# Moving the sums of weight quarters forward in the DMA slots of a hybrid encoder layer, and two small steps on VectorE with them

## The chip, the core and the metric

The kernel runs on one core of a Trainium2 chip. The core has TensorE (matrix products, results in PSUM), VectorE, ScalarE and GpSimd (elementwise work; GpSimd can't read PSUM), and SyncE, whose queue here issues nearly all loads. Each engine works off its own queue strictly in order and waits on semaphores. Transfers that SyncE, ScalarE and GpSimd issue run on the same 16 DMA engines. The metric is the time of one execution on the device, in microseconds.

## What is computed

One step of a hybrid encoder layer for 512 prompt frames and 32 frames of a running stream (544 tokens), width 1024, all in float32, followed by a final norm:

```python
xn = rms_norm(x, g_mix)
u, q, k, v, gates = split(xn @ w_in)
gate_a, gate_b = split(sigmoid(gates + b_gate))
y_pool = (causal_mean_2_4_8_16(u) - u) @ w_pool_grp * pool_scale     # 4 groups of 128 channels
y_sb   = stick_breaking_attention(q, k, v)                            # 8 heads x 64, strictly causal
x = x + (gate_a * (y_pool @ w_pool_up) + gate_b * (y_sb @ w_sb_up)) @ w_out
x = x + square(relu(rms_norm(x, g_mlp) @ w_up)) @ w_down              # hidden width 4096
x = x + sigmoid(rms_norm(x, g_ple) @ w_ple_gate) * (p @ w_ple_proj)
y = rms_norm(x, g_final)
```

## The kernel before

Activations lie with features on partitions and the 544 tokens as columns, in two halves of 272. Every float32 product is made of three products of rounded parts: high x high, low x high and high x low. ScalarE rounds a weight tile (128 x 1024) into `w_hi` (`split`, `hi`, lines 845 and 853), VectorE makes `w_lo` as the difference (1812, 1820). Three tiles are prepared ahead of TensorE, in a ring of four; the raw tiles come through a ring of two buffers in the attention stage and of six later, loaded by SyncE as soon as VectorE has made the low part of the buffer's last tile.

The attention stage is four pairs of heads (`pair`), so eight heads, each over one psum area of scores. For head g, VectorE adds the positive part of the scores to a logarithm ("stick", line 1898), GpSimd masks the four diagonal blocks (`mask_diagonals`, 767), ScalarE rounds, VectorE makes the low part, TensorE forms the sums along keys, ScalarE takes the exponential, GpSimd masks again, the two parts are made again (943, 1919) and TensorE forms the outputs (1420). In the last pair ScalarE has in addition the eight sigmoids of `gate_a` between two changes of its function table, and the rounding of the pooling means. The four pooling groups run through VectorE and ScalarE too: `group_hi` (957) and `group_lo` (1985) empty a result slot in PSUM, and the first pooling product, `pool_part(0)`, uses the slot that group 2 had.

The MLP and the gate after it use Strassen-Winograd products: for each group of weight columns seven products instead of eight. Four of the seven weight tiles are sums of quarters, S1 to S4, which the DMA engines make in device memory: `SUM_STEPS` has four copies in step 0, then two, one and one accumulating transfers in steps 1 to 3, eight transfers for each of 16 groups. `sum_slot(k)` says which groups are at which step in slot k: group i begins in slot i. GpSimd issues slot k's transfers (`sum_copies`, `sum_additions`, lines 782 and 789), for k up to 7 behind the second mask of head k, later when TensorE reaches certain products (`paces`). Before slot k's first transfer it waits until all transfers of the slots before have landed (`sums_made(k - 1)`). SyncE waits, before it loads a sum, until the group's four slots are through.

In the MLP's first group TensorE makes product s = 0 to 6 (A11, S1, S2, S4, S3, A12, A22). ScalarE copies the results of s = 0, 1, 2 out of PSUM (`copy_quarter`, 1097), VectorE adds those of s = 3, 4, 5 (`add_quarter`, 2190) and scales the quarters by the norm's reciprocal root (2214, 2200, 2219). The mean square for that norm is a product with ones (`statistics`, 1657), made behind s = 2; VectorE turns it into a variance (1840), ScalarE takes logarithm and exponential (874, 876, `root`), and VectorE adds a step of Newton (1846 to 1848, `root_step`). Results go through four PSUM slots; product s = 5 writes into the slot of s = 3, once VectorE has added that.

Of the kernel before, what the change touches and what calls it, by code (L numbers as in the profile page):

```python
# [19 lines left out]
HEADS = 8  # L20
# [69 lines left out]
SUM_GROUPS = tuple((what, 2 * c + e) for c in range(CHUNKS) for what in ("up", "dn") if what == "up" or c < SEVENS  # L90
                   for e in range(2)) + (("ple", 0), ("ple", 1))

SUM_PAD = 16

X_QUARTER = {"A11": (0, 0), "S1": (1, 1), "S2": (0, 1), "S4": (0, 1), "S3": (1, 1), "A12": (0, 0), "A22": (1, 0)}
# [17 lines left out]

def stage_results():

    seq = [(("out", q), result_slot(N_OUT + q), False) for q in range(KT)]

    def group(stage, g, pair, stat=None):  # L120
        for s in range(T_UP):
            seq.append(((stage, g, s), 2 * pair + (not IN_X[s]), BY_ACT[s]))
            if s == 2 and stat:
                seq.append(((stat,), 2 * (1 - pair), False))

    for c in range(CHUNKS):
        group("up", 2 * c, 0, "stat1" if c == 0 else None)
        group("up", 2 * c + 1, 1)
        if c < SEVENS:
            seq.extend((("dn", c, s, e), 2 * e + (not IN_X[s]), False) for s in range(T_UP) for e in range(2))  # L130
        else:
            seq.extend((("down", c, q), q % 4, False) for q in range(KT))
    group("ple", 0, 0, "stat2")
    seq.extend((("proj", q), (2 + q) % 4, False) for q in range(KT // 2))

    for what in LAST_ORDER:
        if what[0] == "ple":
            seq.append((what, 2 + (not IN_X[what[2]]), BY_ACT[what[2]]))
        else:
            seq.append((what, {"pj": what[-1], "stat3": 3 * what[-1]}[what[0]], False))  # L140
    return seq
# [156 lines left out]
def hybrid_step_kernel(nc, w_tiles, x_t, p_t, ck_t, cv, state_t, w_grp, vecs,  # L298
# [5 lines left out]
    with ctx:  # L304
# [316 lines left out]

        def sum_slot(k):

            return [(i, k - i) for i in range(max(0, k - len(SUM_STEPS) + 1), min(k + 1, len(SUM_GROUPS)))]

        def sums_made(k):

            return 16 * sum(len(SUM_STEPS[step]) for j in range(k + 1) for _, step in sum_slot(j))
# [8 lines left out]
        def _(sp):  # L637
# [35 lines left out]
            def staged(n):  # L673
                name = STAGED_LOADS[n]
                wait_free(n)
                group, what = group_side(name) or (None, None)
                if what in SUMS:
                    nth = SUM_GROUPS.index(group)
                    sp.wait_ge(sums_in, sums_made(nth + len(SUM_STEPS) - 1))
                    sp.dma_start(raw_buf(n), sums_t[len(SUMS) * nth + SUMS.index(what), :, :])\  # L680
                        .then_inc(raw_in[raw_at(n)], 16)
                elif name[0] == "p":
                    sp.dma_start(raw_buf(n)[:, 0:TOK], p_t[:, name[1], :]).then_inc(raw_in[raw_at(n)], 16)
                else:
                    sp.dma_start(raw_buf(n), w_tiles[stored_tile(name), :, :]).then_inc(raw_in[raw_at(n)], 16)
# [21 lines left out]
        def _(pool):  # L707
# [104 lines left out]
            for c in range(CHUNKS):  # L812
                second = [NTH[("dn", c, s, 0)] for s in (0, 4)] if c < SEVENS else [NTH[("down", c, q)] for q in (0, 4)]
                paces += [(NTH[("up", 2 * c, 0)], NTH[("up", 2 * c + 1, 0)]), tuple(second)]
            for k, (copies, additions) in enumerate(paces, HEADS):
                if copies:
                    pool.wait_ge(full, copies)
                sum_copies(k)
                if copies:
                    pool.wait_ge(full, additions)  # L820
                sum_additions(k)
# [11 lines left out]
        def _(act):  # L833
# [306 lines left out]
            def up_seven(g):  # L1140

                for s in range(T_UP):
# [17 lines left out]
                        act.wait_ge(sum_done, nth_t(g - 1, "T4"))  # L1160
                    if g and s == 2:
                        act.wait_ge(olo_done, nth_lo(g - 1, "T3"))
                    if BY_ACT[s]:
                        copy_quarter(g, n, s)
                    if s == 0 and g % 2 == 1:
# [4 lines left out]
                    if s == 6:  # L1170
                        act.wait_ge(rel_done, 2 * g + 2)
                        square_hi(g, "B11")
                    if g == 0 and s == 3:
                        act.wait_ge(taken, taken_count(NTH[("stat1",)]))
                        root(2)

            def up_group(g):
                for s in range(T_UP):
# [144 lines left out]
        def _(pe):  # L1323
# [337 lines left out]
            def group_of(stage, g, tiles, made_by=None, stat=None, n_squares=0):  # L1661
                for s in range(T_UP):
                    product_of(tiles + s, NTH[(stage, g, s)], s, made_by).then_inc(full, 1)
                    if s == 2 and stat:
                        statistics(stat, n_squares)

            def down(c):
# [131 lines left out]
        def _(dve):  # L1799
# [189 lines left out]
            def pair(i):  # L1989
# [69 lines left out]
                if last:  # L2059
                    group_lo(1)  # L2060
                    mean_lo(2)
                    mean_lo(3)
                    gate(3, i)
                else:
                    split(AHEAD + 7, i, S1_PER)
                stick(1, i)
                if last:
                    group_lo(2)
                    group_lo(3)
                    stick_later(1, i)  # L2070
                    split(AHEAD + 7, i, S1_PER)
# [195 lines left out]

            def group_step(g, s):

                if s == 3 and g == 0:  # L2270
                    statistics("stat1")
                if SIDES[s] in ("S4", "S3", "A12"):
                    add_quarter(g, NTH[("up", g, s)], s)
                if s == 3 and g == 0:
                    root_step(2)
                if SIDES[s] == "S3":
                    scaled_second(g, "S3")
                if SIDES[s] == "A12":
                    scaled_first(g)
# [274 lines left out]
```

## Time and profile before

| | us |
|---|---|
| median of 3 runs | 772.89 |
| lowest, highest | 772.16, 772.94 |
| the profiled execution | 772.34 |
| its span, first to last instruction | 770.6 |

The granted TensorE clock is 0.996 of full speed over the span. The span is what the profile shows; the device time contains 1.7 us more around it. In the rows below an instruction's start is given in us from the start of the span, its length in us, the engine, the line of the kernel, and at the end in brackets how long the engine had been idle and what released it. Consecutive instructions of one kind are one row. DMA shares say how much of the time of all 16 engines the packets of a queue took; overlapping packets can bring a short stretch above 100%.

### The profile page before, as it was taken

The numbers are of one execution on the slowest core, as the hardware profiler recorded it, in microseconds if no ns is written. First come the engines' busy times: TensorE is split into PE (matmuls) and PEld (weight loads), VectorE is DVE, ScalarE is ACT, GpSimd is POOL, SyncE is SP. The second block draws the span as 40 slices with busy tenths as digits, with TensorE's granted clock in tenths as the row PEclk, the third lists the DMA queues.
The fourth block names the chain that finished last, engine by engine and source line by source line (L and its number), as shares of the span: only waits on it lengthen the run. The fifth ranks groups of instructions, "written<-read, shape, count | busy, mean of one in ns | idle before, by whom it ended". The sixth has DMA issues, their size and how long they took to land.

```text
span 770.6 us, 14459 instructions
## 1 busy us (share of the span) xinstructions
PE 754.8 (98%) x5902; PEld 746.2 (97%) x5902; DVE 556.9 (72%) x705; ACT 422.0 (55%) x524; POOL 147.2 (19%) x259
## 2 busy tenths in 40 slices
PE   9999999999999999999999999999999999999994
PEld 9999999999999999999999999999999999999993
DVE  6776556566567527588998669965998667677986
ACT  7545535435485442477674347634763356556575
POOL 1051342453471332021110111111101000000001
PEclk9999999999999999999999999999999999999998
DMA  7254848769779899988797989789776957342503
GB/s 242 93 181 140 233 147 224 225 193 262 218 179 265 259 242 275 292 267 262 213 299 270 236 329 251 282 232 354 207 243 201 278 185 217 105 117 66 204 1 116
DMA packets 49516, 165.78 MB, mean 215 GB/s; under 512 B 6320, under 2 KB 8368, under 8 KB 49456
## 3 DMA queue, kind: packets, MB, share of 16 engines
q1 hardware_dynamic: 28512, 94.16, 35.6%
q0 software_dynamic: 18688, 67.18, 35.5%
q10 hardware_dynamic: 2256, 3.60, 1.4%
q8 instruction: 43, 0.70, 0.4%
q14 instruction: 17, 0.14, 0.1%
HBM read 160.39 MB, written 71.63 MB: 301 GB/s over the span
## 4 chain that ended last, share of the span: by engine, by line
PE 90%; DVE 5%; ACT 3%; issue 1%; DMA 1%; SPq 0%; POOL 0%; POOLq 0%; DVEq 0%
PE psum L1646 23%; PE psum L1697 16%; PE psum L1345 14%; PE psum L1351 14%; PE psum L1348 14%; PE psum L1394 1%; PE psum L1422 1%; DMA xt<-x_t 1%; PE psum L1420 1%; PE psum L1382 1%; PE psum L1381 1%; ACT xt L1265 1%; PE psum L1401 1%; PE psum L1406 1%; ACT L879 0%
## 5 line engine op out<-in xcount | busy, mean ns | idle before, releaser
L853 ACT ACTIVATE w_hi<-raw_more 128x1024 fp32r<-128x1024 f32 x83 | 87.7, 1056 | 72.3 <-PE psum L1697 43.3
L1345 PE MATMUL psum<-a_hi,w_hi 128*128 128x272 f32 x576 | 120.6, 291 | 0.6 <-DVE w_lo L1812 0.5
L1820 DVE TENSOR_TENSOR w_lo<-raw_more,w_hi 128x1024 fp32r<-128x1024 f32 x83 | 101.1, 1222 | 26.1 <-ACT w_hi L853 25.7
L1351 PE MATMUL psum<-a_hi,w_lo 128*128 128x272 f32 x576 | 119.3, 289 | 0.0
L1348 PE MATMUL psum<-a_lo,w_hi 128*128 128x272 f32 x576 | 118.9, 288 | 0.0
L1646 PE MATMUL psum<-u_hi,w_hi 128*128 128x272 f32 x560 | 116.4, 289 | 1.0 <-ACT h_of L1097 1.0
L1646 PE MATMUL psum<-u_hi,w_lo 128*128 128x272 f32 x560 | 115.8, 289 | 0.0
L1646 PE MATMUL psum<-u_lo,w_hi 128*128 128x272 f32 x560 | 115.7, 288 | 0.0
L1345 PEld LDWEIGHTS psum<-a_hi,w_hi 128*128 128x128 f32 x576 | 90.3, 189 | 1.1 <-DVE w_lo L1812 0.7
L1348 PEld LDWEIGHTS psum<-a_lo,w_hi 128*128 128x128 f32 x576 | 90.5, 189 | 0.0
L1351 PEld LDWEIGHTS psum<-a_hi,w_lo 128*128 128x128 f32 x576 | 90.0, 189 | 0.0
L1646 PEld LDWEIGHTS psum<-u_hi,w_hi 128*128 128x128 f32 x560 | 87.9, 188 | 1.7 <-issue 1.2
L1646 PEld LDWEIGHTS psum<-u_lo,w_hi 128*128 128x128 f32 x560 | 88.3, 189 | 0.0
L1646 PEld LDWEIGHTS psum<-u_hi,w_lo 128*128 128x128 f32 x560 | 87.4, 188 | 0.0
L1812 DVE TENSOR_TENSOR w_lo<-raw,w_hi 128x1024 fp32r<-128x1024 f32 x41 | 51.2, 1250 | 43.3 <-ACT w_hi L845 43.1
L1820 DVE TENSOR_TENSOR w_lo<-raw,w_hi 128x1024 fp32r<-128x1024 f32 x44 | 53.6, 1222 | 19.2 <-ACT w_hi L853 12.3
L789 POOL DMA_DIRECT2D sums_t<-sums_t x32 | 27.5, 1013 | 207.1 <-PE psum L1646 87.9
L1348 PE MATMUL psum<-b_lo,w_hi 128*128 128x272 f32 x304 | 62.9, 288 | 0.0
L853 ACT ACTIVATE w_hi<-raw 128x1024 fp32r<-128x1024 f32 x39 | 41.2, 1056 | 36.0 <-PE psum L1697 21.6
L1345 PE MATMUL psum<-b_hi,w_hi 128*128 128x272 f32 x288 | 60.0, 290 | 0.0
L782 POOL DMA_DIRECT2D sums_t<-w_tiles x64 | 33.6, 535 | 135.5 <-DMA sums_t<-w_tiles 97.7
L1351 PE MATMUL psum<-b_hi,w_lo 128*128 128x272 f32 x288 | 59.4, 287 | 0.0
(287 smaller groups left out, 1553.0 us busy)
## 6 DMA issues: line engine op xcount, KB each, us to landing
sums_t<-w_tiles POOLq DMA_DIRECT2D x96, 512.0 KB, 8.2
raw<-w_tiles SPq DMA_DIRECT2D x63, 512.0 KB, 4.4
raw_more<-sums_t SPq DMA_DIRECT2D x42, 512.0 KB, 5.8
raw_more<-w_tiles SPq DMA_DIRECT2D x41, 512.0 KB, 4.5
sums_t<-sums_t POOLq DMA_DIRECT2D x32, 512.0 KB, 11.1
raw<-sums_t SPq DMA_DIRECT2D x22, 512.0 KB, 6.0
xt<-x_t SPq DMA_DIRECT2D x8, 272.0 KB, 5.7
y_t<-xt SPq DMA_DIRECT2D x16, 136.0 KB, 1.9
```

The costliest lines, as they stand in the source:

```text
L782: pool.dma_start(sum_tile(i, what), sum_tile(i, of)).then_inc(sums_in, 16)
L789: pool.dma_start(sum_tile(i, what), sum_tile(i, of), accum_op=ALU.add).then_inc(sums_in, 16)
L853: act.activation(w_hi[:, t % W_RING, :, :].rearrange("p k c -> p (k c)"), src, ACT.Copy)\
L1265: act.activation(x, x, ACT.Copy, scale=g_fin[:, m:m + 1]).then_inc(xg_last, 1)
L1345: pe.matmul(base[:, h, :], w_hi[:, s, wk, :], at(hi, k, h * HALF, (h + 1) * HALF), start=(opens and q == 0), stop=False, skip_group_check= ...
L1348: pe.matmul(base[:, h, :], w_hi[:, s, wk, :], at(lo, k, h * HALF, (h + 1) * HALF), start=False, stop=False, skip_group_check=True)
L1351: mm = pe.matmul(base[:, h, :], w_lo[:, s, wk, :], at(hi, k, h * HALF, (h + 1) * HALF), start=False, stop=(closes and q == len(ks) - 1), s ...
L1381: pe.matmul(z, b_lo[:, keys], b_hi[:, both], start=(b != 3), stop=False, skip_group_check=True)
L1646: mm = pe.matmul(out[:, two, :], w_part[:, t % W_RING, 2 * k + two, :], u_part[:, op, k, :], start=(OPENS[s] and k == 0 and w_part is w_hi ...
L1697: mm = pe.matmul(out[:, two, :], w_part[:, t % W_RING, 2 * k + two, :], h_part[:, i * HALF:(i + 1) * HALF], start=(OPENS[s] and k == 0 and ...
L1812: dve.tensor_tensor(w_lo[:, s, :, :].rearrange("p k c -> p (k c)"), raw[:, t % RAW_RING, :], w_hi[:, s, :, :].rearrange("p k c -> p (k c)" ...
L1820: dve.tensor_tensor(w_lo[:, t % W_RING, :, :].rearrange("p k c -> p (k c)"), src, w_hi[:, t % W_RING, :, :].rearrange("p k c -> p (k c)"), ...
```

## The change

There are three parts.

1. `BEGINS` says in which slot each group of sums begins: 0, 1, 2, 2, 3, 3, 4, 5, 5, 7, 9, 11, 12, 13, 14, 15. Nine groups instead of six begin in slots 0 to 5. SyncE's wait for a group follows it.
2. In the last pair, `group_lo(2)` stands ahead of the last stick instead of behind it.
3. The mean square of the MLP's norm is made behind s = 1. ScalarE's root stands ahead of its copy of S2's result, VectorE's variance at the end of s = 2, and `root_step(2)` ahead of the addition of S4's result.

```diff
+BEGINS = (0, 1, 2, 2, 3, 3, 4, 5, 5, 7, 9, 11, 12, 13, 14, 15)
+SLOTS = BEGINS[-1] + len(SUM_STEPS)
...
+STAT_BEHIND = {"stat1": 1, "stat2": 2}
...
-            if s == 2 and stat:
+            if s == STAT_BEHIND.get(stat):
...
-            return [(i, k - i) for i in range(max(0, k - len(SUM_STEPS) + 1), min(k + 1, len(SUM_GROUPS)))]
+            return [(i, k - at) for i, at in enumerate(BEGINS) if 0 <= k - at < len(SUM_STEPS)]
...
-                    sp.wait_ge(sums_in, sums_made(nth + len(SUM_STEPS) - 1))
+                    sp.wait_ge(sums_in, sums_made(BEGINS[nth] + len(SUM_STEPS) - 1))
...
-            for k, (copies, additions) in enumerate(paces, HEADS):
+            for k, (copies, additions) in zip(range(HEADS, SLOTS), paces):
...
+                    if g == 0 and s == 2:
+                        act.wait_ge(taken, taken_count(NTH[("stat1",)]))
+                        root(2)
                     if BY_ACT[s]:
                         copy_quarter(g, n, s)
...
-                    if g == 0 and s == 3:
-                        act.wait_ge(taken, taken_count(NTH[("stat1",)]))
-                        root(2)
...
+                if last:
+
+                    group_lo(2)
                 stick(1, i)
                 if last:
-                    group_lo(2)
                     group_lo(3)
...
+                if s == 2 and g == 0:
+                    statistics("stat1")
                 if s == 3 and g == 0:
-                    statistics("stat1")
+                    root_step(2)
                 if SIDES[s] in ("S4", "S3", "A12"):
                     add_quarter(g, NTH[("up", g, s)], s)
-                if s == 3 and g == 0:
-                    root_step(2)
```

GpSimd from the second mask of head 4 to the issue of slot 5, in the kernel before. `sums_t` holds the sums; a transfer from `w_tiles` on the first DMA line is a copy, those on the second are additions; `gates` and `upad` are the window mean:

```order
L767 AFFINE_SELECT work<-work 128x128 x4
L782 DMA sums_t<-w_tiles 128x1024 x4
L789 DMA sums_t<-sums_t 128x1024 x2
L789 DMA sums_t<-w_tiles 128x1024 x2
L757 TENSOR_SCALAR gates<-gates 128x551
L758 TENSOR_TENSOR gates<-gates,invc 128x8
L760 TENSOR_TENSOR upad<-gates,upad 128x559
L767 AFFINE_SELECT work<-work 128x128 x8
L782 DMA sums_t<-w_tiles 128x1024 x4
L789 DMA sums_t<-sums_t 128x1024 x2
L789 DMA sums_t<-w_tiles 128x1024 x2
```

and in the changed one, with the line numbers moved by 8:

```order
L775 AFFINE_SELECT work<-work 128x128 x4
L790 DMA sums_t<-w_tiles 128x1024 x4
L797 DMA sums_t<-sums_t 128x1024 x3
L797 DMA sums_t<-w_tiles 128x1024 x4
L765 TENSOR_SCALAR gates<-gates 128x551
L766 TENSOR_TENSOR gates<-gates,invc 128x8
L768 TENSOR_TENSOR upad<-gates,upad 128x559
L775 AFFINE_SELECT work<-work 128x128 x8
L790 DMA sums_t<-w_tiles 128x1024 x8
L797 DMA sums_t<-sums_t 128x1024 x4
L797 DMA sums_t<-w_tiles 128x1024 x2
```

Slot 4 grows from 4 copies and 4 additions to 4 and 7, slot 5 to 8 and 6 (the other slots of the first eight follow from `BEGINS`).

ScalarE at the MLP's first group. `w_hi` is a weight rounding, `h_of` the copy of a result, `ev` logarithm and exponential. Before:

```order
L853 ACTIVATE w_hi<-raw 128x1024
L1097 ACTIVATE h_of<-psum 128x2x272
L853 ACTIVATE w_hi<-raw 128x1024
L1097 ACTIVATE h_of<-psum 128x2x272
L853 ACTIVATE w_hi<-raw_more 128x1024
L874 ACTIVATE ev<-work 128x544
L876 ACTIVATE ev<-ev 128x544
L853 ACTIVATE w_hi<-raw_more 128x1024 x2
```

and now:

```order
L861 ACTIVATE w_hi<-raw 128x1024
L1105 ACTIVATE h_of<-psum 128x2x272
L861 ACTIVATE w_hi<-raw 128x1024
L882 ACTIVATE ev<-work 128x544
L884 ACTIVATE ev<-ev 128x544
L1105 ACTIVATE h_of<-psum 128x2x272
L861 ACTIVATE w_hi<-raw_more 128x1024 x3
```

The two functions moved ahead of the copy and of the rounding of the tile for s = 6.

VectorE at the same place, before (`w_lo` a weight's low part, `work<-psum` the variance, `ev` and `rn` the step of Newton, `h_of` with `psum` an addition of a result):

```order
L1820 TENSOR_TENSOR w_lo<-raw,w_hi 128x1024 x2
L1820 TENSOR_TENSOR w_lo<-raw_more,w_hi 128x1024
L1840 TENSOR_SCALAR work<-psum 128x544
L2190 TENSOR_TENSOR h_of<-h_of,psum 128x2x272
L1846 SCALAR_TENSOR_TENSOR ev<-ev 128x544
L1847 TENSOR_TENSOR ev<-ev,work 128x544
L1848 SCALAR_TENSOR_TENSOR rn<-ev 128x544
L1820 TENSOR_TENSOR w_lo<-raw_more,w_hi 128x1024
L2190 TENSOR_TENSOR h_of<-h_of,psum 128x2x272
L2214 SCALAR_TENSOR_TENSOR h_of<-h_of,rn 128x2x272
```

and now:

```order
L1828 TENSOR_TENSOR w_lo<-raw,w_hi 128x1024 x2
L1848 TENSOR_SCALAR work<-psum 128x544
L1828 TENSOR_TENSOR w_lo<-raw_more,w_hi 128x1024
L1854 SCALAR_TENSOR_TENSOR ev<-ev 128x544
L1855 TENSOR_TENSOR ev<-ev,work 128x544
L1856 SCALAR_TENSOR_TENSOR rn<-ev 128x544
L2200 TENSOR_TENSOR h_of<-h_of,psum 128x2x272
L1828 TENSOR_TENSOR w_lo<-raw_more,w_hi 128x1024
L2200 TENSOR_TENSOR h_of<-h_of,psum 128x2x272
L2224 SCALAR_TENSOR_TENSOR h_of<-h_of,rn 128x2x272
```

The variance moved ahead of one low part, and the three steps of the root ahead of the first addition.

## Rows read from the trace of the kernel before

**Rows 1.** the page's part 1: busy us, share of the span, instructions
```profile
PE 754.8 (98%) x5902; PEld 746.2 (97%) x5902; DVE 556.9 (72%) x705; ACT 422.0 (55%) x524; POOL 147.2 (19%) x259
```

**Rows 2.** instructions in order of time, TensorE; [idle before <-releaser] at the end
```profile
245.09 0.49 PE L1345 MATMUL psum<-mean_hi,w_hi 128*128 128x272 f32 x2 [1.11 <-issue]
...
384.42 0.49 PE L1646 MATMUL psum<-u_hi,w_hi 128*128 128x272 f32 x2 [1.02 <-ACT h_of L1097]
```

**Rows 3.** in order of time, GpSimd, 139 to 229 us (L767: masks)
```profile
140.45 2.15 POOL L782 DMA_DIRECT2D sums_t<-w_tiles  x4
...
169.95 2.09 POOL L782 DMA_DIRECT2D sums_t<-w_tiles  x4
...
174.18 2.92 POOL L757 TENSOR_SCALAR gates<-gates 128x551 f32<-128x551 f32 x1
...
183.69 1.03 POOL L767 TENSOR_SCALAR_AFFINE_SELECT work<-work 128x128 f32<-128x128 f32 x4 [5.16 <-DVE work L1898]
...
210.60 1.95 POOL L767 TENSOR_SCALAR_AFFINE_SELECT work<-work 128x128 f32<-128x128 f32 x4 [6.14 <-DVE work L1898]
```

**Rows 4.** DMA queues (q0 GpSimd's, q1 SyncE's): 260:262, 152:156, 162:170, 140:170 us
```profile
q0 software_dynamic: 206, 0.76, 101.1%
...
q0 software_dynamic: 237, 0.84, 107.5%
...
q0 software_dynamic: 40, 0.01, 0.8%
...
q0 software_dynamic: 1216, 4.21, 57.0%
q1 hardware_dynamic: 576, 2.10, 20.2%
```

**Rows 5.** in order of time, ScalarE, 212 to 229 us
```profile
212.58 1.27 ACT L930 ACTIVATE b_hi<-work 128x1280 fp32r<-128x1280 f32 x1 [2.62 <-POOL work L767]
...
228.41 1.27 ACT L943 ACTIVATE b_hi<-work 128x1280 fp32r<-128x1280 f32 x1 [0.19 <-POOL work L767]
```

**Rows 6.** stretch: us, ScalarE busy (x instructions), clock, DMA share, GB/s
```profile
214.10:228.20 14.10, 13.91 (x20) 1.00 0.62 166
```

**Rows 7.** in order of time, VectorE, then TensorE, 230 to 233 us
```profile
230.81 1.48 DVE L1919 TENSOR_TENSOR b_lo<-work,b_hi 128x1280 fp32r<-128x1280 f32 x1
...
232.67 0.39 PE L1420 MATMUL psum<-b_hi 128*128 128x512 f32 x1
```

**Rows 8.** in order of time, GpSimd, then TensorE, 267 to 269 us
```profile
267.74 0.44 POOL L807 TENSOR_SCALAR_AFFINE_SELECT work<-work 32x256 f32<-32x256 f32 x1 [6.18 <-DVE work L2111]
...
268.34 0.59 PE L1559 MATMUL psum<-work,negtri 128*128 128x256 f32 x2
```

**Rows 9.** in order of time, VectorE, then ScalarE, 242 to 246 us
```profile
242.82 1.48 DVE L1898 SCALAR_TENSOR_TENSOR work<-psum,work 128x1280 f32<-128x1280 f32 x1
244.21 1.47 DVE L1985 SCALAR_TENSOR_TENSOR b_lo<-psum,vec,b_hi 128x544 fp32r<-128x544 f32 x2
...
242.93 0.72 ACT L957 ACTIVATE b_hi<-psum,vec 128x544 fp32r<-128x544 f32 x1 [0.74 <-PE psum L1328]
```

**Rows 10.** in order of time, VectorE, then ScalarE, 361 to 376 us
```profile
362.56 2.36 DVE L1820 TENSOR_TENSOR w_lo<-raw,w_hi 128x1024 fp32r<-128x1024 f32 x2
366.10 1.23 DVE L1820 TENSOR_TENSOR w_lo<-raw_more,w_hi 128x1024 fp32r<-128x1024 f32 x1 [1.19 <-ACT w_hi L853]
367.24 0.72 DVE L1840 TENSOR_SCALAR work<-psum 128x544 f32<-128x544 f32 x1
...
369.38 0.73 DVE L1846 SCALAR_TENSOR_TENSOR ev<-ev 128x544 f32<-128x544 f32 x1 [0.16 <-ACT ev L876]
...
373.55 0.72 DVE L2214 SCALAR_TENSOR_TENSOR h_of<-h_of,rn 128x544 f32<-128x544 f32 x1
...
365.02 1.05 ACT L853 ACTIVATE w_hi<-raw_more 128x1024 fp32r<-128x1024 f32 x1
368.00 0.66 ACT L874 ACTIVATE ev<-work 128x544 f32<-128x544 f32 x1 [1.93 <-DVE work L1840]
```

More of the change, by code:

```diff
@@ L1663, in group_of @@
                     product_of(tiles + s, NTH[(stage, g, s)], s, made_by).then_inc(full, 1)
-                    if s == 2 and stat:
+                    if s == STAT_BEHIND.get(stat):
                         statistics(stat, n_squares)
```

## The prediction, made before the changed kernel ran

> **What bounds the kernel now.** Read the busy shares first: TensorE is busy 98% of the span, VectorE 72%, ScalarE 55%, GpSimd 19% [rows 1]. So a change can only give back one of TensorE's few gaps, or open new ones. Then TensorE's waits, and for the two of about 1 us that aren't at the start or the end its rows in order of time [rows 2]: 1.11 us in front of the first product after the last attention pair (start 245.09), 1.02 us in front of a product of the second MLP group (start 384.42). The second and third part of the change can be worth these two gaps, 2.1 us or 0.27%, and no more. The first part, the sums of weight quarters begun earlier, frees no engine that TensorE waits for; its gain can only be zero, and what it can cost has to be looked for on GpSimd's queue, since the copies and additions are issued there, between the masks that attention needs.
>
> **First part: sums begun earlier.** The 128 transfers stay the same; they move between slots. By the start numbers the slots 0 to 7 hold 4, 6, 11, 14, 11, 14, 7 and 7 transfers, where they held 4, 6, 7, 8, 8, 8, 8 and 8. GpSimd begins slot k behind the second mask of head k, and first waits until every transfer of slots before k has landed. A slot is one head long: slot 3 is begun at 140.45, slot 4 at 169.95, 29.5 us later [rows 3].
> What a transfer takes: when only copies are in the queue, 0.76 MB move in 2 us at a 101% share of the 16 DMA engines [rows 4], so the 0.524 MB of one take 1.38 us. When only additions are in it, 0.84 MB move in 4 us at a share over 100%, so one takes 2.5 us, 2.6 with the ragged ends. The engines are full in both cases, so more transfers in the queue don't make them faster. Over the 30 us of slot 3 GpSimd's queue took 57% and the weight loads 20% of the engines, and it was empty from 162.3 on (0.01 MB after 162) [rows 4]. That is 21.85 us from 140.45, which leaves 7.6 us to spare.
> Slot 3 in the new order has 4 copies and 2 additions more: 4 x 1.38 + 2 x 2.6 = 10.7 us of engine time; with the loads taking a fifth of the engines (0.21) that is 10.7 / 0.79 = 13.5 us. It ends at 162.3 + 13.5 = 175.8 where GpSimd asks at 169.95. GpSimd is held for 5.85 us. Slot 4 has 3 additions more, 7.8 / 0.79 = 9.9: it ends at 175.8 + 21.85 + 9.9 = 207.55. Slot 5 then issues 14 transfers; eight took 4.23 us (169.95 to 174.18 [rows 3]), 0.53 each, so 7.4 us: GpSimd is free for the next mask at 214.95.
> Behind the waiting instruction stand the masks. At head 5 the mask is due at 183.69 [rows 3]; GpSimd would come to it at 175.8 + 11 x 0.53 = 181.6, and a window mean of some 4 us stands in between (it begins behind the last issue, at 174.18 before): about 2 us late. Some of it reaches TensorE, an estimated 0.8 us, since the outputs of head 5 use the masked values one head later with less than that to spare. At head 6 it is due at 210.60 [rows 3] and comes at 214.95. The mask ended at 212.55 and ScalarE took it up at 212.58 after 2.62 us of waiting; alone on the SBUF it takes about 1.0 us (four selects) and ends at 215.95, 3.4 us late. From there ScalarE has no air: of the 14.1 us up to 228.2 it is busy 13.91 [rows 6], with eight sigmoids and two table loads, and what follows, the rounding of the probabilities at 228.41, waited for nothing but 0.19 us of mask [rows 5]. VectorE's low part of them starts at 230.81, takes 1.49, and TensorE reads it at 232.67 [rows 7]: 0.4 us to spare. So 3.0 us of the 3.4 arrive at TensorE; the 0.8 of head 5 is contained in them, since this chain hangs on GpSimd's time and not on TensorE's.
> Slot 5 (14 transfers again) ends at 207.55 + 21.85 + 13.5 = 242.9. Slot 6 is 7 additions: 18.2, and 6 for start and loads (21.85 less 4 x 1.38 + 4 x 2.6), and about 2.2 for the 1 MB of cached keys and values loaded in it, so it ends near 269.3. Slot 7's issue takes 7 x 0.53 = 3.7 more: 273.0. The mask of the running stream's scores, due at 267.74, is read by TensorE at 268.34 [rows 8]. It will be due at 267.74 + 3.0 - 0.5 = 270.25 and comes 2.75 later; 0.15 is slack: 2.6 us. After that no work of GpSimd's is awaited until the end, and the fuller slots are over. Together 5.6 us. Bounds: with 2.4 us an addition and 1.3 a copy the head 6 term is 1.1 and the other 0; with 2.8 and 1.5 and 25% for the loads it is 7.2 and the other up to 4. I take the middle, because the rates come from this same stretch.
> Weight loads beside a busy queue land later, but [rows 4] has the engines as full in stretches where TensorE runs on; I cost this at 0, at most 0.6.
> What is relieved lies in the later stages, where TensorE had no gap: 0.
> A page differs here. The Trainium skill, "DMA: Bandwidth & Descriptors", section on the anatomy of one DMA, fits a GpSimd-issued DMA as 2.0 us plus bytes / 436 GB/s, 1.2 us for 0.524 MB, for additions as for copies; by it 14 transfers would be through in about 19 us and the loads would not carry them beyond the head. The trace disagrees for additions (2.5 us, [rows 4]), and the row decides.
>
> **Second part: the third group's mean.** TensorE's first product after the pair needs the PSUM slot that VectorE's L1985 for group 2 empties. It stands behind the stick (242.82, 1.48 long) and starts at 244.21; ScalarE's half of it starts at 242.93 and takes 0.7 [rows 9]. Ahead of the stick it can start at 243.69, 0.52 earlier; TensorE follows by 0.5. Its gap was 1.1 [rows 2], so 0.6 stays: the group's own product is next. Behind it the stick and its mask end 1.5 later (0.87 of it because the group's own rounding isn't done before 243.65). What hid them is the two products of 3 us that TensorE has before it asks for the sticks' low parts, at 251.1 before and 250.6 now; VectorE's four steps behind the mask (three short additions, a weight split, the low part, the carried low part) end at about 250.7. The cover is used up, but not exceeded by over 0.1. Taken: -0.5 (bounds -0.6 and +0.5).
>
> **Third part: the norm's sums one product sooner.** TensorE's two matmuls run at once, the squares are added. But VectorE is busy with two weight splits from 362.56 to 364.84 [rows 10], so the variance starts at 364.84, not at 361. ScalarE's logarithm follows 0.76 after it, as before (367.24, 368.00) [rows 10]. Now the order bites: behind logarithm and exponential comes the copy of S2's result, and only then the weight rounding, which before stood at 365.02 ahead of the root. 364.84 + 0.76 + 1.77 (three short functions) = 367.37. VectorE's split of that tile starts 1.08 later, at 368.45 instead of 366.10, and the root's steps stand behind it: 369.59 instead of 369.38. Before, from there to the scaled quarter were 4.17 us (373.55 - 369.38) [rows 10]; now the addition of S4's result lies in it as well, 0.64. The scaled quarter starts at 374.40, 0.85 us late, and the chain from it to the 1.0 us gap in [rows 2] is unbroken. The gap doesn't close; it is 0.85 us of loss. (The product after S3 also waits some 1.2 us for that addition's PSUM slot, but inside the same delay.) Bounds: +1.3 and, if ScalarE had the rounding done in time, -1.0. Taken: +0.85.
>
> **Sum.** 5.6 - 0.5 + 0.85 = 5.95 us. The profiled execution took 772.34 us (span 770.6), 0.55 below the median of the runs, 772.89. So 778.8 us on the median's scale.
>
> **The rivals.** A measurement here tells about 0.2% (1.5 us) from no change.
> (1) *The slots drain in time.* If transfers overlapped better in a fuller queue, as by the page's fit, GpSimd isn't held, and the other two parts remain: +0.35, 773.2 us. For it: TensorE's path is untouched where POOL is early, and slot 3 alone had 7.6 us to spare. Against: shares at 100% in both kinds of stretch. Chance 0.16.
> (2) *It does what it says.* Slots drain, the mean gives 0.5, and the earlier statistics close the 1.0 us gap: 771.3 us, 0.2% faster. It needs a ScalarE that rounds the tile before VectorE asks; the order speaks against it. 0.12.
> (3) *It is worse than the sum.* The held masks add up, by slower additions or by GpSimd blocked while it issues 14 transfers in a row (no slot before has over 8, so none shows what the queue does with 14): from 11 us on, 784 to 790. 0.10.
> (4) *Forecast*, GpSimd held at slots 4, 5 and 7: 774 to 784, likeliest 778.8. 0.62.
> That the sums aren't begun earlier after all is excluded: the order of GpSimd's instructions shows it.
>
> **Numbers.** Faster 0.12, same 0.16, slower 0.72. The range takes the forecast with both bounds and case 1: 772.6 to 784.5.
>
> **What would show it.** In the trace after, GpSimd's wait on its own DMAs before slot 4's copies (none before; 5.9 us), before slot 5's (8) and before slot 7's; the masks of heads 5 and 6 starting later than the stick that feeds them; new TensorE gaps near 204, 220 to 238 and 270 us, released by masks or low parts. With those absent case 1 or 2 holds. For the third part: the time from the variance to the scaled quarter grown from 6.3 us (367.24 to 373.55) to some 9.5, and the gap in the second group still there; if it is gone, my order on ScalarE is wrong. For the second: TensorE's gap in front of the pooling products at 0.6. I would be wrong most easily in the end of slot 4: 3 us earlier, and the head 6 term is gone.

## The result and the profile after

The changed kernel takes 799.6 us (median of 6 runs, 798.35 to 800.72), against 773.88 us for the kernel before (median of the 6 runs beside it, 772.16 to 776.51): 1.033 of the time before, 95% interval 1.030 to 1.035. The forecast was 778.8 us, in a range up to 784.5. The direction was right, the size was missed by 21 us. The profiled execution has a span of 799.0 us, 28.4 more than before. Of the kernel before, one of the executions timed beside the experiments below took 1491.5 us; it enters no ratio.

The page, parts 1 and 2, the kernel after (40 slices of 20 us; before, TensorE had 98% [rows 1]):

```profile
PE 761.1 (95%) x5902; PEld 750.5 (94%) x5902; DVE 557.4 (70%) x705; ACT 422.4 (53%) x524; POOL 146.5 (18%) x259
...
PE   8999999999792999999999999999999999999993
...
PEclk9999999999896999999999999999999999999997
```

TensorE's busy time grew by 6 us although its work is the same. It has one slice (240 to 260 us) in which it hardly ran, and two slices with a lower granted clock. Its waits say for what:

```profile
engine line waited for: us in total, times, longest us
PE psum L1334 <- DVE mean_lo L1988: 13.8, 1, 13.8
PE psum L1428 <- DVE b_lo L1927: 5.5, 3, 4.6
```

Two gaps, of 13.8 and 4.6 us, where the longest outside start and end had been 1.1 [rows 2]. To attribute the whole loss I compared the starts of TensorE's 5902 matmuls one by one, in order. The difference between the two traces changes only at a few places, so it can be read to a tenth of a microsecond, which the total can't. Late means later than in the kernel before:

```
place (us, before)    lateness, before -> behind it   step
  6 and 57              0.00 -> 0.95                 +0.95  start and first head
203 to 206              0.95 -> 8.21                 +7.26  outputs of head 5
218                     8.21 -> 8.81                 +0.60
232 to 236              8.81 -> 26.22               +17.41  the last attention pair
245                    26.22 -> 25.68                -0.54  pooling products
251                    25.68 -> 25.88                +0.20  sticks of the last head
361 to 366             25.88 -> 26.33                +0.45  the norm's sums
371                    26.33 -> 27.38                +1.05  product behind S3
384                    27.38 -> 26.69                -0.69  the old gap of 1.02
end                    26.7
```

The other 1.7 us of the span lie behind the last matmul and differ between executions (spans of this kernel: 796.6 to 799.0).

**The chain of the 13.8 us gap**, GpSimd in order of time:

```profile
204.26 1.03 POOL L775 TENSOR_SCALAR_AFFINE_SELECT work<-work 128x128 f32<-128x128 f32 x4 [12.69 <-ACT work L946]
214.24 4.19 POOL L790 DMA_DIRECT2D sums_t<-w_tiles  x8 [8.95 <-DMA sums_t<-w_tiles]
...
220.57 2.96 POOL L797 DMA_DIRECT2D sums_t<-w_tiles  x2
221.63 2.92 POOL L775 TENSOR_SCALAR_AFFINE_SELECT work<-work 128x128 f32<-128x128 f32 x4
226.36 0.64 POOL L750 DMA_DIRECT2D pool_t<-upad  x1 [1.80 <-DVE upad L1981]
...
235.44 0.22 POOL L766 TENSOR_TENSOR gates<-gates,invc 128x16 f32<-128x16 f32 x1
250.66 1.18 POOL L768 TENSOR_TENSOR upad<-gates,upad 128x559 f32<-128x559 f32 x1 [15.01 <-DMA pool_t<-upad]
```

GpSimd is held for 8.95 us in front of slot 5, as forecast (8). But the mask of head 6 (221.63) isn't what TensorE ends up waiting for. Behind it GpSimd issues two stores of 15 columns of pooling state (L750, L751), forms the window sums, and then waits 15.01 us for these two stores before it may overwrite `upad` with the mean (L768, behind `pool.wait_ge(pool_out, 32 * (g + 1))`). They are 7.5 KB each. VectorE makes `mean_lo` from the mean, and TensorE's product at 254.67 waits for that. The DMA issues from 214 to 250 us show why the stores take so long (count, KB each, median us to landing):

```profile
sums_t<-w_tiles POOLq DMA_DIRECT2D x10, 512.0 KB, 10.1
sums_t<-sums_t POOLq DMA_DIRECT2D x4, 512.0 KB, 20.7
...
v_t<-ev ACTq DMA_DIRECT2D x1, 272.0 KB, 7.7
pool_t<-upad POOLq DMA_DIRECT2D x2, 7.5 KB, 23.0
```

ScalarE's store of 272 KB lands in 7.7 us in the same stretch, from its own queue. The tiny ones, issued behind the 14 of slot 5 in GpSimd's queue, land in 23.0. Before, the same eight stores (all four groups) landed in 2.2, 5.5 and 8.0 us (least, median, most), and the mean at 223.72 found them done; after, in 2.2, 12.5 and 23.5. Of the tile `pool_t`, the kernel before, then after:

```profile
DMA to landing us min/median/max: 2.2/5.5/8.0
```

```profile
DMA to landing us min/median/max: 2.2/12.5/23.5
```

**The clock.** The granted clock in the stretches around both gaps (us, TensorE, weight loads, VectorE, ScalarE, GpSimd busy, clock, DMA share, GB/s):

```profile
204.00:206.00 2.00, 0.00 (x0) 0.00 (x0) 0.69 (x1) 1.92 (x3) 1.03 (x4) 1.00 1.03 264
206.00:208.00 2.00, 0.00 (x0) 0.00 (x0) 1.90 (x2) 0.60 (x1) 0.00 (x0) 0.65 1.08 312
208.00:210.00 2.00, 1.82 (x5) 1.63 (x6) 0.94 (x3) 0.00 (x0) 0.00 (x0) 0.50 1.06 249
210.00:212.00 2.00, 2.00 (x9) 1.81 (x8) 1.14 (x2) 0.00 (x0) 0.00 (x0) 0.50 0.84 287
...
246.00:248.00 2.00, 0.00 (x0) 0.00 (x0) 0.00 (x0) 0.00 (x0) 0.00 (x0) 0.50 1.09 222
...
258.00:260.00 2.00, 2.00 (x10) 2.00 (x10) 0.62 (x2) 0.00 (x0) 1.81 (x3) 0.50 1.05 207
```

TensorE was at its upper level (2.4 GHz) until it had stood still for some 3 us, then at the lower (0.50, 1.2 GHz), and still there when work came back: 9 or 10 matmuls in 2 us, where the kernel before has 15 to 18 in the same places. That is why a gap of 4.57 us became a step of 7.26 and one of 13.81 a step of 17.41: 2.7 and 3.6 us more.

**Third part**, VectorE in order of time, after (answers to [rows 10], 25.9 us later by then):

```profile
390.72 0.72 DVE L1848 TENSOR_SCALAR work<-psum 128x544 f32<-128x544 f32 x1
394.31 1.23 DVE L1828 TENSOR_TENSOR w_lo<-raw_more,w_hi 128x1024 fp32r<-128x1024 f32 x1 [2.87 <-ACT w_hi L861]
395.45 0.72 DVE L1854 SCALAR_TENSOR_TENSOR ev<-ev 128x544 f32<-128x544 f32 x1
...
400.25 0.73 DVE L2224 SCALAR_TENSOR_TENSOR h_of<-h_of,rn 128x544 f32<-128x544 f32 x1
```

The variance is 2.4 us sooner (390.72 - 25.88 = 364.84), and VectorE then stands idle for 2.87 us until ScalarE has rounded the tile it put behind the root. From variance to scaled quarter: 9.53 us.

### The profile page after: what moved, and what is told of

Read it like the earlier page. It is cut to its first block, busy times and chain, and to the rows that moved or that the text cites. A ratio compares the mean times of both kernels' runs of the same rounds, so it can differ in the third digit from the quotient of the medians.

```text
span 799.0 us, 14458 instructions
## 1 busy us (share of the span) xinstructions
PE 761.1 (95%) x5902; PEld 750.5 (94%) x5902; DVE 557.4 (70%) x705; ACT 422.4 (53%) x524; POOL 146.5 (18%) x259
## 4 chain that ended last, share of the span: by engine, by line
PE 68%; DMA 12%; issue 6%; DVE 5%; POOL 4%; ACT 3%; POOLq 0%; ACTq 0%; SPq 0%; DVEq 0%
PE psum L1654 22%; PE psum L1705 16%; PE psum L1353 8%; PE psum L1359 8%; PE psum L1356 8%; DMA sums_t<-w_tiles 8%; DMA pool_t<-upad 3%; DMA raw<-w_tiles 2%; POOL sums_t L797 1%; POOL sums_t L790 1%; DVE w_lo L1820 1%; ACT xt L1273 1%; PE psum L1402 1%; POOL work L775 1%; PE psum L1428 1%
## 5 line engine op out<-in xcount | busy, mean ns | idle before, releaser
L797 POOL DMA_DIRECT2D sums_t<-sums_t x32 | 27.3, 1066 | 261.3 <-PE psum L1654 93.7
L861 ACT ACTIVATE w_hi<-raw 128x1024 fp32r<-128x1024 f32 x39 | 41.2, 1057 | 36.0 <-PE psum L1705 21.7
L853 ACT ACTIVATE w_hi<-raw 128x1024 fp32r<-128x1024 f32 x46 | 48.2, 1052 | 18.5 <-DMA raw<-w_tiles 9.6
```

Source lines behind the costliest of these rows:

```text
L797: pool.dma_start(sum_tile(i, what), sum_tile(i, of), accum_op=ALU.add).then_inc(sums_in, 16)
L853: act.activation(w_hi[:, s, :, :].rearrange("p k c -> p (k c)"), raw[:, t % RAW_RING, :], ACT.Copy).then_inc(whi_done, 1)
L861: act.activation(w_hi[:, t % W_RING, :, :].rearrange("p k c -> p (k c)"), src, ACT.Copy)\
```

## The experiments

Steps in TensorE's start times, here too, are read against the kernel before. A ratio stands with its 95% interval. But for the one execution named above, the kernel before ranged from 772.2 to 776.8 us beside these runs, so a single run says little below 3 us, and its trace says more.

**sums_alone.** Only `BEGINS` and its uses, on the kernel before.

```diff
+BEGINS = (0, 1, 2, 2, 3, 3, 4, 5, 5, 7, 9, 11, 12, 13, 14, 15)
...
-            return [(i, k - i) for i in range(max(0, k - len(SUM_STEPS) + 1), min(k + 1, len(SUM_GROUPS)))]
+            return [(i, k - at) for i, at in enumerate(BEGINS) if 0 <= k - at < len(SUM_STEPS)]
```

> Only the first part: the sums begun earlier, both other parts as before. Theory Q (the two small stores of the pooling state, issued by GpSimd, stand in its DMA queue behind the 14 transfers of slot 5, and the window mean waits for them): the gap of 13.8 us ahead of the last pair's products and the 4.6 us gap at head 5 both stay, about 799 us (798 to 801), TensorE 26 us later than before from 260 us on. Rival R (the moved mean and root add to the loss, or cause it): under 795 us.

798.8 us, ratio 1.033 (1.030 to 1.036). Steps of +7.50 at 203 and +15.27 at 232, gaps of 4.6 and 11.9 us with the same releasers, and one of +1.1 at 195 (a gap of 0.82, waiting for VectorE's `later_lo`) that the changed kernel's trace doesn't have. The first part is the whole loss.

**stores_apart.** The changed kernel, the stores' source copied to a tile of its own.

```diff
-                pool.dma_start(pool_t[0, :, g, :], u[:, U_STATE - STATE:U_STATE]).then_inc(pool_out, 16)
+                link(pool.tensor_copy(kept[:, g % 2, 0:STATE], u[:, U_STATE - STATE:U_STATE]))
...
+                pool.dma_start(pool_t[0, :, g, :], kept[:, g % 2, 0:STATE]).then_inc(pool_out, 16)
...
-                pool.wait_ge(pool_out, 32 * (g + 1))
```

> The changed kernel with the 2 x 15 columns of pooling state copied to a tile of their own on GpSimd and stored from there, so that the window mean doesn't wait for the stores; all transfers in the same slots. Theory Q: the 13.8 us gap and the half clock behind it (17.4 us together) go; what the late masks of head 6 cost (3 us by my forecast) may come in their place: 782 to 786 us. The gap of 4.6 us at head 5 stays. Rival (full DMA engines slow everything that TensorE needs there, the weight loads above all): another gap of over 8 us near 245 us, time over 790.

797.3 us, ratio 1.030 (1.028 to 1.033): the time missed the expectation by more than 10 us, though the gap went as expected; the rival's time came, without its gap of over 8 us. Against the changed kernel only 2.3 us of the median came back. The trace (span 792.7, the fastest of its four runs) has the mean at 236.66 without a wait. The step at 232 fell from 17.41 to 5.63, but behind it a new one of 5.38 opened, where there had been none:

```profile
PE psum L1432 <- DVE b_lo L1931: 6.5, 3, 4.5
PE psum L1548 <- DMA cvn<-cv: 2.1, 1, 2.1
```

L1548 is the running stream's product with the cached keys. ScalarE issues the loads of cached keys and values (`ckt`, `cvn`), and they now run beside GpSimd's full queue. So the 13.8 us gap had covered for a third loss: while TensorE stood still, the queue had emptied. The 5.63 us are two gaps of 1.22 and 1.01 us at 242 and 244, and the clock at 0.50 from 244 to 250.

**slots_2_to_4.** Slots of 4, 6, 11, 14, 7, 4, 6 transfers, otherwise the kernel before.

```diff
+BEGINS = (0, 1, 2, 2, 3, 3, 6, 7, 8, 9, 10, 11, 12, 13, 14, 15)
```

> The kernel before with slots 2 and 3 as full as in the change (11 and 14 transfers) and slots 4 to 6 lighter (7, 4, 6). Theory: two losses that are apart. Head 5's alone is left: GpSimd asks for slot 4 at 170 us, gets it at 179, TensorE has a gap of some 4.6 us near 203 and less than full clock behind it, 7.3 us in all: 780 to 781 us, no gap at 241. Rival (the fuller queue costs through shared DMA engines, wherever it is full): 774 to 777 with small gaps in many places.

777.4 us (one run). One large step, +5.22 at 203, with a gap of 3.37 us; none at 232. The time alone wouldn't tell the two apart; the trace does. It has the theory's place and releaser, 2 us smaller: the mask of head 5 starts at 187.88, 1.2 us sooner against TensorE than in the change (4.7 us late instead of 5.9; 7 issues stand ahead of it instead of 11), and the clock stayed low for 3.4 us instead of 6.8.

**slot_5_alone.** 16 transfers in slot 5, slots 0 to 4 as before.

```diff
+BEGINS = (0, 1, 2, 3, 4, 5, 5, 5, 8, 9, 10, 11, 12, 13, 14, 15)
```

> The kernel before with 16 transfers in slot 5 (12 copies, 4 additions; 27 us of engine time as the change's slot 5 has) and slots 0 to 4 as before. Theory Q: head 5 has no gap; the stores of group 3's state, issued at 214.3, land when slot 5 is through, at about 233 (198.9 + 34.5); the mean, the second mask and the rounding behind it come 8 us late; a gap of about 8 us near 230 to 242, with the clock's fall some 11: 782 to 786 us. Rival C (the 15 us wait of the mean grew only out of head 5's delay): no gap, 773 us.

785.7 us (one run), as expected by theory Q. The stores land some 5 us later than worked out (at 238.5, not 233), and the gap is 2 us longer for it:

```profile
215.40 0.56 POOL L745 DMA_DIRECT2D pool_t<-upad  x1
...
238.60 1.18 POOL L762 TENSOR_TENSOR upad<-gates,upad 128x559 f32<-128x559 f32 x1 [14.54 <-DMA pool_t<-upad]
```

One step, +13.18 at 232, with a gap of 10.2 us ahead of `mean_lo`. Head 5 has no gap, so this loss is not a child of the first.

**slot_5_apart.** The same, with the state stored from its own tile, as in stores_apart.

> The kernel of slot_5_alone (16 transfers in slot 5, slots 0 to 4 as before), with the pooling state stored from a tile of its own so that the mean doesn't wait for the stores. Theory Q (the 13.2 us of slot_5_alone came from the mean's wait for two stores in GpSimd's queue, and from nothing else that is full there): the mean is computed by 226, the second mask at 228; no gap near 232, TensorE within 0.5 us of the kernel before up to 250, time 773 to 775. Rival L (with the queue full up to 237, weight loads and cached keys land late): gaps of 2 us or more between 200 and 265 with landing named as their cause, time 776 or more.

781.8 us, ratio 1.0086 (1.0057 to 1.0116). Both sides were right for a part of it. Up to 261 us TensorE's lateness is flat (0.48 us, from the start): the step of 13.18 at 232 is gone with the wait for the stores, and nothing else that is full at that time costs anything. Then rival L's gap comes, at the cached keys:

```profile
267.94 2.40 PE L1542 MATMUL psum<-qbd,ckt 128*128 128x64 f32 x10 [6.03 <-DMA cvn<-cv]
```

It is worth 9.60 us with its clock. The loads were issued at 254.2 and 254.9, as before (254.4), and took 9.1 and 13.0 us to land, where they had taken 4.1 and 5.1; slot 6's eight additions, issued at 238.73 because slot 5 had held them, landed at 269.1. Tile `cvn`, the kernel before, then this one:

```profile
DMA to landing us min/median/max: 5.1/5.1/5.1
```

```profile
DMA to landing us min/median/max: 13.0/13.0/13.0
```

**mean_first.** stores_apart with two steps of GpSimd exchanged. The exchange holds for heads 0, 2 and 4, so it also moves head 2's mean ahead of slot 2.

```diff
+                if g % 2 == 0 and g != HEADS - 2:
+                    window_mean(g // 2, sums)
                 sum_copies(g)
                 sum_additions(g)
-                if g % 2 == 0 and g != HEADS - 2:
-                    window_mean(g // 2, sums)
```

> As stores_apart, with the window mean of a head ahead of the slot's transfers instead of behind them, so that it is computed while GpSimd waits for slot 3's landing. Theory: of the 5.9 us by which head 5's mask is late, some 5 are the mean behind 11 issues; the mask comes at about 185.5 + the offset of 1 us and the gap of 4.5 us near 203 falls to under 1 us (6.4 us with its clock becomes under 1.5). Head 6's 5.6 us and the 5.4 us at the cached keys stay: 788 to 793 us. Rival (the late landing itself, 179.4 instead of 170.9, makes the gap): the gap stays at over 3 us.

798.9 us (one run). The gap at head 5 is 4.82 us as ever (+7.07), so the expected time and gap didn't come. But the run doesn't test the mean alone, since GpSimd now waits 3.47 us in front of slot 3, where it waited for nothing in the change:

```profile
144.04 4.12 POOL L794 DMA_DIRECT2D sums_t<-w_tiles  x8 [3.47 <-DMA sums_t<-w_tiles]
...
181.40 2.15 POOL L794 DMA_DIRECT2D sums_t<-w_tiles  x4 [7.09 <-DMA sums_t<-w_tiles]
...
185.14 4.34 POOL L801 DMA_DIRECT2D sums_t<-w_tiles  x4
187.25 3.27 POOL L779 TENSOR_SCALAR_AFFINE_SELECT work<-work 128x128 f32<-128x128 f32 x4
```

Slot 2 was issued behind head 2's mean and landed later, so slot 3 was issued at 144.04 instead of 141.58. It took 37.4 us, as in the change (37.9), and landed at 181.40, against TensorE 2.8 us later than in the change. The last of the 11 issues ends at 189.48 (185.14 + 4.34), and the mask 1.04 us behind it. In the change the mean ended 3.1 us behind its last issue (187.50 to 190.59), and that is what the exchange saved; the later landing took it back. The masks end at 190.5, 5.8 us late, as in the change (5.9). So the mean is a part of what makes the mask late, of about 3 us, and the landing is the larger one. Further steps here are +4.4 at 218 (a gap of 2.63 us and the lower clock), +1.2 at 232, +1.1 at 251, and +10.77 at the cached keys.

**order_alone, round_first, norm_kept_on_pe.** The sums in their old slots; the second part in all three. order_alone has the third part as in the change. round_first takes back ScalarE's order:

```diff
-                    if g == 0 and s == 2:
-                        act.wait_ge(taken, taken_count(NTH[("stat1",)]))
-                        root(2)
                     if BY_ACT[s]:
                         copy_quarter(g, n, s)
...
+                    if g == 0 and s == 3:
+                        act.wait_ge(taken, taken_count(NTH[("stat1",)]))
+                        root(2)
```

norm_kept_on_pe takes back TensorE's too (`STAT_BEHIND = {"stat1": 2, "stat2": 2}`), and keeps VectorE's.

> The second and third part without the first: the sums in their old slots. By the trace of the changed kernel these parts are worth -0.54 and +0.20 us (the third group's mean ahead, the sticks' low parts after it) and +0.45, +1.05, -0.69 us (the norm's sums): +0.5 us in all, which the clock can't tell from nothing: 772.5 to 775, verdict same; in TensorE's start times the same five steps in the same places. Rival (in the changed kernel they were masked by the idle time before them): the steps differ.

> As order_alone, but ScalarE rounds the seventh product's weight tile ahead of the norm's logarithm and exponential, as in the kernel before. Theory (the third part's 0.8 us come from that order alone): VectorE's split comes at 366.1 instead of 368.5, the root's steps 2 us sooner, the addition of S4's result frees its PSUM slot in time (no 0.84 us gap) and the 1.0 us gap of the second MLP group closes: TensorE 0.9 us ahead of the kernel before at the end instead of 0.5 us behind it; time 772 to 773.5. Rival: the sums one product sooner cost TensorE by themselves, then nothing is gained against order_alone.

> As round_first, but TensorE computes the sums where it did before, behind the third product; only VectorE takes the variance ahead of the next split and the root's steps ahead of the addition. Theory: variance done 0.1 us after that of round_first is still ahead of the split, so the gap closes as well, and TensorE doesn't wait for the squares (0.45 us): 1.3 us ahead of the kernel before at the end. Rival: without the sooner sums the root comes behind S4's result and the gap stays, TensorE 0.3 us ahead (from the second part alone).

```
                  ratio (95%)               245    251    361-366  371    384
order_alone       0.9989 (0.9973-1.0005)   -0.49  +0.20   +2.28   +1.06  -0.69
round_first       0.9987 (0.9967-1.0007)   -0.54  +0.19   +0.46   +0.19  -0.69
norm_kept_on_pe   0.9973 (0.9957-0.9989)   -0.53  +0.21    0       0     -1.14
```

order_alone's steps are those of the change, in the same places, but for one: +2.28 instead of +0.45 at the norm's sums, and +1.15 ahead of it. round_first has TensorE's order too and neither of these; one_group_sooner (below) has TensorE's order of before and two such steps (+0.72, +1.68). So they don't follow TensorE's order; with one trace of each kernel, what makes them is open. round_first was half right: the step at 371 fell from 1.05 to 0.19, but the gap at 384 didn't close any further, and what remains is the price of the sooner sums, 0.46 us on TensorE, against a gain of 0.69. norm_kept_on_pe came out as expected, with no price. VectorE in order of time:

```profile
365.34 0.72 DVE L1848 TENSOR_SCALAR work<-psum 128x544 f32<-128x544 f32 x1 [0.42 <-PE psum L1665]
366.02 1.23 DVE L1828 TENSOR_TENSOR w_lo<-raw_more,w_hi 128x1024 fp32r<-128x1024 f32 x1
367.48 0.72 DVE L1854 SCALAR_TENSOR_TENSOR ev<-ev 128x544 f32<-128x544 f32 x1 [0.23 <-ACT ev L884]
...
372.28 0.72 DVE L2224 SCALAR_TENSOR_TENSOR h_of<-h_of,rn 128x544 f32<-128x544 f32 x1
```

The variance fills an idle moment ahead of the split, the root's steps fill one ahead of S4's result, and the scaled quarter comes at 372.28 instead of 373.55 [rows 10]. At 0.9973 (median 772.04 us) this version is 0.3% faster than the kernel before, and the interval leaves out 1.

**one_group_sooner.** Each group from the fourth on begun one slot sooner: 4, 6, 11, 10, 9, 9, 8, 8 transfers.

```diff
+BEGINS = (0, 1, 2, 2, 3, 4, 5, 6, 7, 8, 9, 10, 11, 12, 13, 14)
```

> The kernel before with every group from the fourth on begun one slot sooner: slots of 4, 6, 11, 10, 9, 9, 8, 8 transfers. Theory (a fuller slot costs nothing as long as it has landed when GpSimd asks for the next and when the mean asks for its stores): slot 2 (8 copies, 3 additions, 19 us of engine time) lands before 140.5, slot 5 has 9 with 8.4 us to the stores, which land one copy later (224 to 226 instead of 222) and hold the mean by 0 to 2 us, within its slack of some 3 us; time 772 to 775, TensorE's starts as before within 0.5 us. Rival L: each fuller slot costs something, 1 us or more in all.

775.65 us, ratio 1.0008 (0.9995 to 1.0021). The 11 transfers of slot 2 land in time. Slot 5 has one more, and the mean already feels it:

```profile
226.97 1.18 POOL L762 TENSOR_TENSOR upad<-gates,upad 128x559 f32<-128x559 f32 x1 [3.49 <-DMA pool_t<-upad]
```

The wait of 3.49 us (2 expected at most) reaches TensorE as +0.68 us at 233. So the kernel before stood close to this edge: with its slot of 8 the stores landed some 1.5 us before the mean at 223.72 (7.6 us after their issue, median).

## Why the prediction was wrong, and where it was right

**What bounds, and which part can cost.** Right: the first part gives nothing and costs on GpSimd's queue, all of it. The price list of that queue was incomplete.

**The term that was missing: the gap of 13.8 us.** The prediction walked GpSimd's instructions past the fuller slots and asked for each when its engine would be free. It saw the masks as the only thing awaited, and took the window mean for 4 us of computing. It did not ask what the mean itself waits for: two stores that go into the same DMA queue behind slot 5. The trace of before had it to read: 7.5 KB took up to 8.0 us to land, with nothing waiting for it. With the prediction's own drain of slot 5 (242.9) these stores land at 243 and the mean, due at 224, is 19 us late; the term would have been found. stores_apart and slot_5_apart show that the wait is the cause (the step of 13.18 goes to nothing), slot_5_alone that it needs neither slot 3 nor slot 4. But the 17.4 us of that step are not what the wait costs by itself. Without it (stores_apart) TensorE's last start is 20.4 us late instead of 26.7, since other losses come up in its place (head 6 and the running stream, below). So this term is not the whole miss. The Trainium skill, "DMA: Bandwidth & Descriptors", section on queues, rings and completion order, says that each of the 16 engines consumes a queue's descriptors in ring order and takes turns between the queues. The trace agrees with both: 23.0 us for 7.5 KB behind the sums in GpSimd's queue, 7.7 us for 272 KB from ScalarE's beside them.

**Head 5: 0.8 us forecast, 7.26 measured.** The mechanism was right, three sizes were low. GpSimd in the changed kernel:

```profile
179.44 2.10 POOL L790 DMA_DIRECT2D sums_t<-w_tiles  x4 [8.48 <-DMA sums_t<-w_tiles]
...
190.54 1.03 POOL L775 TENSOR_SCALAR_AFFINE_SELECT work<-work 128x128 f32<-128x128 f32 x4
```

Slot 3 landed at 179.44, with TensorE 0.95 late by then, against 175.8: the 14 transfers took 37.9 us, not 35.4. The mask ended 5.9 us late, not 2: behind that landing stand 11 issues (5.8 us) and a mean that ran 5.3 us and not 4 behind them. Of the 5.9 us, 4.57 reach TensorE, as 3.37 of 4.7 do in slots_2_to_4: the slack was 1.3 us, and "some of it reaches TensorE" was no working. And 2.7 us are the clock.

**The clock was left out.** The prediction had no term for it. In the runs a still TensorE fell to the lower level each time it stood for 3.37 us or more, and the work behind the gap ran at half speed. So it did after lone gaps of 2.07 (stores_apart) and 2.63 us (mean_first), and after two of 1.22 and 1.01 that followed each other (stores_apart). The step was 1.8 to 4.3 us larger than the gap each time. Lone gaps of 1.0 to 2.03 us didn't do it (clock 1.00 in order_alone around its gap of 2.03).

**Head 6 and the running stream: 3.0 + 2.6 forecast.** In the changed kernel neither can be seen, since the stores' wait stands in their place and its idle time drains the queue. With that wait gone they show: 5.63 us at head 6 (2.2 of gaps, and the clock), and 5.4 to 10.8 us at the running stream. That the gaps at head 6 are near the forecast 3.0 is in part luck: slot 4 landed at 214.24 and not at 207.55, and the mask of head 6 ended 12.0 us later than before and not 3.4, but TensorE was 8.8 us late by then, where the forecast had 0.8. At the running stream the place and the moment were right and the waited-for thing was wrong: not the mask, but the cached keys and values, which the prediction had counted only as 2.2 us of load on the queue. Loads beside a busy queue were costed at 0, at most 0.6; that step failed. It held for the weights, for which TensorE, past its start, has no new wait of 0.3 us or more in any of these runs, and not for the loads that are issued 7 us before their use (254.4 and 261.3 in the kernel before).

**Rival 1 (slots drain in time).** Excluded: slots 3 and 4 took 37.9 and 34.8 us, longer than a head. By the fit in the Trainium skill, "DMA: Bandwidth & Descriptors", section on the anatomy of one DMA, whose part for the bytes is 1.2 us for 0.524 MB, 14 transfers would take an estimated 19 us; the trace disagrees. Rival 3, "worse than the sum", was the case that happened, in its direction; the mechanism it named (blocked by the issuing) is only a small part: the mask behind the issues ends 1.9 to 2.2 us later than its start would have it.

**Second part: -0.5 forecast, -0.54 measured**, in three more kernels -0.49 to -0.54. Its "cover not exceeded by over 0.1" came to +0.20 at 251 in each.

**Third part: +0.85 forecast, +0.81 measured** (+0.45, +1.05, -0.69). The order on ScalarE was the decisive point, as said: variance 364.84 forecast and measured, scaled quarter 374.40 forecast, 400.25 - 25.88 = 374.37 measured. How it is spread was wrong: the addition's wait is a step of its own of 1.05, and the gap at 384 shrank to 0.34 because TensorE came to it later. The bound of -1.0 "if ScalarE had the rounding done in time" didn't come: round_first has the rounding in time, and its steps add up to -0.04 (+0.46, +0.19, -0.69). Only with TensorE's order of before as well, in norm_kept_on_pe, was it -1.14; the prediction had no term for what the sooner product with ones costs on TensorE, 0.45 us.

## What to carry to other kernels

Before filling a DMA queue further, list everything that goes through the same queue, however small, and who waits for each; here a 7.5 KB store behind 7.3 MB landed after 23.0 us. When a fuller queue delays one thing, look for the next thing behind it too: here the wait for the stores hid the wait for the cached keys, by giving the queue time to drain, and taking it away gave back 2.3 us of 25.7. And on a kernel whose TensorE never rests, price a new gap with its clock too: in these runs the lower clock put 1.8 to 4.3 us on top of gaps of 2.07 us and more, while the clock stayed at 1.00 over one of 2.03.

## What the hardware showed that was not expected

GpSimd's first instruction behind a row of DMA issues has a longer record. Four masks take 1.03 us; directly behind 14 issues 2.92 (221.63, above), behind 11 issues 3.27 (mean_first). In both the record of the last issues runs on beneath it, to 223.53 and 189.48, and the masks end 1.02 and 1.04 us after that. So by these records it is the issuing that lasts longer than the distance of the starts says: 9.3 us for 14, 8.1 us for 11, where the prediction had 7.4 and 5.8.

A load of another queue beside a full queue of GpSimd's takes up to 2.6 times as long: `cvn` took 5.1 us before, 6.5 in the changed kernel (where the queue had drained), 9.1 in stores_apart, 13.0 in slot_5_apart and 13.4 in mean_first.
